# First layer's modulation tiles on VectorE and ScalarE, and branch D attention as three products of split operands

## What is computed

```
def modulate(h, shift, scale):
    return h * (1 + scale) + shift
...
        s = jnp.einsum('bhgqd,bhkd->bhgqk', qi, k).astype(jnp.float32) * scale
        p = jax.nn.softmax(s, axis=-1).astype(v.dtype)
        return jnp.einsum('bhgqk,bhkd->bhgqd', p, v)
...
    y = dense_block_attention(q, jnp.concatenate([kc, k], axis=2), jnp.concatenate([vc, v], axis=2), scale)
...
    for l in range(DEPTH):
        mod = jnp.split((sc @ ada_w[l] + ada_b[l])[:, None, :], 6, axis=-1)
        mod_c = jnp.split(scc @ ada_w[l] + ada_b[l], 6, axis=-1)
        h = modulate(rmsnorm(x, norm1_w[l]), mod[0], mod[1])
...
        x = x + mod[2] * gated_merge([ya, yb, yg, yd], p[4], w_branch[l], w_o[l])
        x = x + mod[5] * sqrelu_mlp(modulate(rmsnorm(x, norm2_w[l]), mod[3], mod[4]), mlp_w1[l], mlp_w2[l])
```

## Time and profile before

| | us |
|---|---|
| median of three runs | 2999.7 |
| their range | 2998.19 to 2999.82 |
| the profiled execution | 3000.03 |
| its span, first to last instruction | 2998.2 |

### The profile page before, as it was taken

How to read it: one execution, slowest core, us unless ns; L and a number is a source line. 1 busy time by engine, 2 the same in 40 slices (tenths; PEclk the granted TensorE clock), 3 DMA queues, 4 the chain that set the end, 5 groups by cost and what they waited for, 6 DMA issues and landing times. The chain is left out here.

```text
span 2998.2 us, 38375 instructions
## 1 busy us (share of the span) xinstructions
PE 2828.2 (94%) x15368; PEld 2308.8 (77%) x15368; DVE 1502.5 (50%) x2348; ACT 1233.9 (41%) x2155; POOL 165.9 (6%) x188
## 2 busy tenths in 40 slices
PE   6999999999999999999999999999998899999998
PEld 4887786778778778888888878777566676788887
DVE  4258753446553445664344443873446544554444
ACT  4434434434553443544233344443445544442222
POOL 0022210000000000000000000230000000000000
PEclk8999999999999999999999999999999999999999
DMA  5122231032222223243333232224031130423332
GB/s 207 57 101 96 92 138 54 22 105 76 75 84 78 67 95 120 92 141 113 112 112 112 78 107 71 84 85 138 11 96 50 43 102 22 151 85 98 93 97 91
DMA packets 84817, 273.59 MB, mean 91 GB/s; under 512 B 9520, under 2 KB 9776, under 8 KB 83888
## 3 DMA queue, kind: packets, MB, share of 16 engines
q1 hardware_dynamic: 74896, 229.84, 23.6%
q0 software_dynamic: 9760, 41.50, 4.3%
HBM read 245.07 MB, written 26.22 MB: 90 GB/s over the span
## 5 line engine op out<-in xcount | busy, mean ns | idle before, releaser
L717 PE MATMUL slot<-Hh,wh 128*128 128x512 f32 (+1 forms) x2384 | 869.9, 366 | 30.6 <-DVE wl L1849 9.2
L717 PE MATMUL slot<-Hh,wl 128*128 128x512 f32 (+1 forms) x2384 | 836.1, 352 | 0.0
L717 PE MATMUL slot<-Hl,wh 128*128 128x512 f32 (+1 forms) x2384 | 835.5, 351 | 0.0
L717 PEld LDWEIGHTS slot<-Hh,wh 128*128 128x128 f32 x2384 | 452.7, 190 | 99.0 <-issue 25.8
L1849 DVE TENSOR_TENSOR wl<-raw,wh 128x1024 fp32r<-128x1024 f32 (+1 forms) x332 | 379.6, 1144 | 289.2 <-ACT wh L1328 286.5
L1328 ACT ACTIVATE wh<-raw 128x1024 fp32r<-128x1024 f32 (+1 forms) x332 | 323.2, 974 | 435.8 <-PE slot L717 356.5
L717 PEld LDWEIGHTS slot<-Hh,wl 128*128 128x128 f32 x2384 | 452.0, 190 | 61.5
L717 PEld LDWEIGHTS slot<-Hl,wh 128*128 128x128 f32 x2384 | 453.2, 190 | 58.6 <-issue 6.0
L717 PE MATMUL slot<-Uh,wh 128*128 128x512 f32 (+1 forms) x776 | 273.9, 353 | 0.0
L717 PE MATMUL slot<-Ul,wh 128*128 128x512 f32 (+1 forms) x776 | 273.4, 352 | 0.0
L717 PE MATMUL slot<-Uh,wl 128*128 128x512 f32 (+1 forms) x776 | 273.0, 352 | 0.0
(11 more groups left out here) (258 smaller groups left out, 3847.1 us busy)
## 6 DMA issues: line engine op xcount, KB each, us to landing
raw<-w_dram SPq DMA_DIRECT2D x204, 512.0 KB, 3.5
raw<-w_gate_dram SPq DMA_DIRECT2D x64, 512.0 KB, 3.6
ada_g_raw<-ada_dram POOLq DMA_DIRECT2D x48, 512.0 KB, 3.8
ada_g_raw<-ada_dram SPq DMA_DIRECT2D x32, 512.0 KB, 3.8
raw<-w_merge_dram SPq DMA_DIRECT2D x64, 256.0 KB, 2.8
g_kept<-logits_out SPq DMA_DIRECT2D x32, 384.0 KB, 2.3
SS<-g_kept SPq DMA_DIRECT2D x32, 384.0 KB, 3.6
ada_first<-ada_dram SPq DMA_DIRECT2D x8, 1024.0 KB, 17.8
```

The costliest lines, as they stand in the source:

```text
L717: return pe.matmul(dst, lhsT, rhs, start=start, stop=stop)
```

## The change

First, `modulation_in`, `later_ada_out` and `last_column` go. Layer 0's 32 later tiles are made as layer 1's are: a product on DVE (`first_layer_product`, 128x2048) and two sums on ACT (`first_layer_sum`). They stand at the jobs of `ADA_JOBS`: ten of the C projection, the eight of the D projection, seven out-projection jobs and the first group's steps 2 to 8. The product is the first thing in DVE's `begin_job`, ahead of `low`; the sums stand behind `high` in ACT's. The condition's rows (`cs_rows`) are brought by POOL three times. Layer 1's 16 tiles of the first group move to its steps 8 to 15: one at step 8, three at step 12, two at the others.

Second, branch D's attention products are made from split operands. ACT makes high parts of each q, k and v, DVE low parts (`split_into_high`, `low_of_d`, `v_low`), and each plain product becomes three fp32r ones. Of each unit of turned probabilities ACT's copy is the high part and a new DVE subtraction, which reads the PSUM bank, the low one (`PT_LOW`, 72 units in both layers: 64 of 384 columns, 8 of 256). It stands at the head of DVE's iteration, and it, not the copy, frees the bank.

```
-        ada_prod = [at(f"ada_prod{k}", [2, D_MODEL], f32, (R_S + 7) * ROW + k * 2 * D_MODEL * 4) for k in range(2)]
+        ada_prod = [at(f"ada_prod{k}", [2, D_MODEL], f32, (R_S + 4) * ROW + (k + 1) * 2 * D_MODEL * 4) for k in range(2)]
...
-        PT["D"] = PT["B"]
+        PT["D"] = at("PT_D", [NB, SEQ], f32r, (R_S + 7) * ROW)
+        PT_LOW = [at(f"PT_low{k}", [NB // 2, SEQ], f32r, first * ROW) for k, first in enumerate((R_S, R_X + 6))]
+        KD_HIGH, KD_LOW = rows("KD_high", R_X + 2, D_KV, f32r), rows("KD_low", R_X + 4, D_KV, f32r)
+        VD_HIGH = rows("VD_high", R_X, D_KV, f32r)
+        VD_LOW = [rows(f"VD_low{k}", row, 1, f32r)[:, 0, :] for k, row in enumerate((R_S + 11, R_S + 2))]
...
-        ADA_STEPS = {"first": [x for x in range(2, 2 * KT) for _ in range(2 if x in (9, 12) else 1)],
+        FIRST_D = sum(N_PROJ[b] + LATER_GATES[0][b] + KT for b in BRANCHES[:-1])
+        ADA_JOBS = list(range(2, 10)) + [11, 12] + list(range(FIRST_D, FIRST_D + KT)) + list(range(FIRST_FF - KT, FIRST_FF - 1))
+        ADA_JOBS += list(range(FIRST_FF + 2, FIRST_FF + KT + 1))
+        assert len(ADA_JOBS) == N_GATE
+
+        ADA_STEPS = {"first": [x for x in range(KT, 2 * KT) for _ in range({KT: 1, 12: 3}.get(x, 2))],
...
                 tile(src, raw, raw_full, jobs % 2, size)
+                if jobs - 1 in ADA_JOBS:
+                    ada_tile(ADA_JOBS.index(jobs - 1))
...
+            def ada_tile(t):
+
+                sp.wait_ge(ada_read.sem, ADA_FIRST + max(t - 1, 0))
+                sp.dma_start(ada_g_raw[t % 2][:, :, :], w_ada[ADA_FIRST + t]).then_inc(ada_g_full[t % 2].sem, 16)
...
-                        if j > 0:
-                            ada_tile(layer, len(gate_jobs) - 2)
...
-                        if x == 0:
-                            ada_tile(layer, len(gate_jobs) - 1)
...
+            def condition_rows():
+
+                rows_in = cs_kept.rearrange("s p k -> s (p k)").unsqueeze(0).to_broadcast([P, 2, D_MODEL])
+                pool.dma_start(cs_rows[:, :, :], rows_in).then_inc(cs_back.sem, 16)
...
+                if layer == 0:
+                    pool.wait_ge(cs_packed.sem, w.next(cs_packed))
+                    for side in range(2):
+                        pool.dma_start(cs_kept[side], cs[:, side * KT:(side + 1) * KT]).then_inc(cs_saved.sem, 16)
+                    pool.wait_ge(cs_saved.sem, w.next(cs_saved, 2))
+                    pool.wait_ge(mod_done.sem, w.next(mod_done, FIRST_PIECES))
+                    condition_rows()
...
+                        if layer == 0 and after == BRANCHES[-1]:
+                            condition_rows()
...
-                            pool.dma_start(cs_rows[:, :, :], rows_in).then_inc(cs_back.sem, 16)
+                            condition_rows()
...
-            def modulation_in(dst, full, tile):
-
-                pe.wait_ge(full.sem, w.next(full))
-                for k in range(KT):
-                    strip = slice(32 * (k % 4), 32 * (k % 4 + 1))
-                    last = mm(dst[strip, :], cs_wide[:, k, :], tile[:, k, :], start=k < 4, stop=k >= 4)
-                last.then_inc(ada_read.sem, 1)
...
-                    if part == 1:
-                        modulation_in(later_ada, ada_g_full[g % 2], ada_g_raw[g % 2])
-                        if g > 0:
-                            mm(later_cols, mod_g_t[(g - 1) % 2][:, :], sel)
...
-                        transposes(beside, slot[beside], VT[branch][j % 2], NB, copied).then_inc(tr_done.sem, 1)
+                        transposes(beside, slot[beside], VT[branch][j % 2], NB, v_low if branch == "D" else copied).then_inc(tr_done.sem, 1)
...
+                            if branch == "D" and tile["first"] and len(tile["keys"]) == NB and h % (D_HEADS // D_KV) == 0:
+                                pe.wait_ge(d_low.sem, w.next(d_low, 1 if h else D_SPLITS - 1))
...
-                                    last = mm(out_s[:, lo:hi], QY[:, h, qs_], KD[:, h // (D_HEADS // D_KV), lo:hi])
+                                    kv = h // (D_HEADS // D_KV)
+                                    mm(out_s[:, lo:hi], Yh[:, h, qs_], KD_HIGH[:, kv, lo:hi], start=True, stop=False)
+                                    mm(out_s[:, lo:hi], Yl[:, h, qs_], KD_HIGH[:, kv, lo:hi], start=False, stop=False)
+                                    last = mm(out_s[:, lo:hi], Yh[:, h, qs_], KD_LOW[:, kv, lo:hi], start=False, stop=True)
...
-                        pe.wait_ge(pt_ready.sem, w.next(pt_ready, values_in))
+                        pe.wait_ge(turned.sem, w.next(turned, values_in))
+                        if branch == "D" and i - LAG - 1 == LB - 1:
+                            pe.wait_ge(v_low.sem, w.next(v_low, D_KV))
...
-                                last = mm(values_at[:, 0:tile["width"]], V[:, tile["h"] // 2, m * P:(m + 1) * P], pt, **flags)
+                                kv, block = tile["h"] // (D_HEADS // D_KV), slice(m * P, (m + 1) * P)
+                                dst, low = values_at[:, 0:tile["width"]], PT_LOW[x // 3][:, x % 3, 0:tile["width"]]
+                                mm(dst, VD_HIGH[:, kv, block], pt, start=x == 0, stop=False)
+                                mm(dst, VD_LOW[kv][:, block], pt, start=False, stop=False)
+                                last = mm(dst, VD_HIGH[:, kv, block], low, start=False, stop=flags["stop"])
...
-                            pe.wait_ge(*slots.next(("unit", units % 2), pt_ready))
+                            pe.wait_ge(*slots.next(("unit", units % 2), turned))
...
-                if layer == 0 and branch == BRANCHES[-1]:
-                    last_column()
...
+                first_layer_sum(layer, n)
...
-                    if layer == 0:
-                        later_ada_out(later)
...
+                    if branch == "D":
+                        dst = Yh[:, j, 0:nq] if kind == "q" else KD_HIGH[:, j, :]
+                        act.activation(dst, src[:, 0:nq] if kind == "q" else src, ACT.Copy).then_inc(d_high.sem, 1)
+                        return
...
+                        split_before = branch == "B" and n > 0 or branch == "D" and n > 2
+                        p = begin_job(between=(lambda: split_into_high(*plan[n - (3 if branch == "D" else 1)])) if split_before else None)
...
+                        if branch == "D":
+                            act.activation(VD_HIGH[:, j, :], slot[beside][:, 0:T], ACT.Copy).then_inc(v_high.sem, 1)
...
+                    split_into_high(*plan[D_SPLITS - 1])
...
+            def first_layer_sum(layer, n):
+
+                if layer or n not in ADA_JOBS:
+                    return
+                t = ADA_JOBS.index(n)
+                act.wait_ge(ada_read.sem, w.next(ada_read, 1 + (0 if t else ADA_FIRST)))
+                for side in range(2):
+                    row = ada_prod[t % 2][:, side, :]
+                    ins = act.activation(row, row, ACT.Copy, accum_out=mod[:, ADA_FIRST + t, side:side + 1])
+                ins.then_inc(ada_summed.sem, 1)
+
...
+                        if first:
+                            first_layer_sum(layer, n + x)
...
+                first_layer_product(layer, n)
                 if n > min(layer, 1):
...
+                        if branch == "D" and n > 2:
+                            between = lambda: low_of_d(nq, *plan[n - 3])
...
+                    if branch == "D" and n > 0 and plan[n - 1][0] == "v":
+                        j = plan[n - 1][1]
+                        dve.wait_ge(v_high.sem, w.next(v_high))
+                        dve.tensor_tensor(VD_LOW[j], slot[1 + 2 * ((n - 1) % 2)][:, 0:T], VD_HIGH[:, j, :].bitcast(f32),
+                                          ALU.subtract).then_inc(v_low.sem, 1)
+                if branch == "D":
+                    low_of_d(nq, *plan[D_SPLITS - 1])
+
+            def low_of_d(nq, kind, j):
+
+                dve.wait_ge(d_high.sem, w.next(d_high))
+                if kind == "q":
+                    ins = dve.tensor_tensor(Yl[:, j, 0:nq], QY[:, j, 0:nq], Yh[:, j, 0:nq].bitcast(f32), ALU.subtract)
+                else:
+                    ins = dve.tensor_tensor(KD_LOW[:, j, :], KD[:, j, :], KD_HIGH[:, j, :].bitcast(f32), ALU.subtract)
+                ins.then_inc(d_low.sem, 1)
...
+                    if branch == "D" and LAG < i <= len(tiles) + LAG:
+                        tile = tiles[i - LAG - 1]
+                        for lo, hi in key_units(tile):
+                            span = slice(tile["col"], tile["col"] + P)
+                            dve.wait_ge(pt_high.sem, w.next(pt_high))
+                            dve.tensor_tensor(PT_LOW[lo // 3][:, 0:hi - lo, span],
+                                              unit_bank(units)[:, 0:(hi - lo) * P].rearrange("p (b s) -> p b s", s=P),
+                                              PT["D"][:, lo:hi, span].bitcast(f32), ALU.subtract).then_inc(pt_low.sem, 1)
+                            units += 1
                     for j, part in over:
...
```

(20 more changed lines are left out.)

113 lines of the change are left out of this document (40 added, 73 removed).

## The result

The change made the kernel slower by 0.33%, where the prediction had 2992.4 us and a range up to 3004.

The account below looks back on a forecast made before the run. The prediction took PE, busy for 94% of the span, as the bound. C -7.8, A -2.3, B -5.5, last column -0.2, D +1.6 and +2.5, feed-forward +4.4 gave -7.3, so 2992.4 us, range 2977 to 3004.

Parts of the forecast that it names:

- The sum by its own terms: All predicted changes of the whole kernel's time added up: -7.3 us.
- 9 of 17 gates paying: Branch C: modulation off PE saves time only in gates not followed by a PE wait; C -7.8 us in all.
- my 2.3 and 5.5: Modulation taken off PE saves 2.3 us in branch A and 5.5 us in branch B.
- The ring: Branch D attention: ACT's exponential and copies, DVE's subtractions and row maximum form a loop of 3.56 us a tile.
- the later start: Branch D: first scores come later through added products, sums and splits, +4.1 us in layer 0, +1.1 in layer 1.
- my +2.5: Branch D attention of layer 1, later start included: +2.5 us.
- +1.4: Layer 0 from D to out-projection: +1.6 us for D, -0.2 for the last column.
- +4.4: First feed-forward group: steps fall behind through the moved products, +4.4 us, bounds 1 and 8.
- The slower one: Rival in D attention: each subtraction costs the ring more, at 0.80 us D gives +23.1, time 3011 us; chance 0.10.
- The third: Rival: half of the modulation's gain of 15.6 us is off the path, time 3000.2 us; chance 0.20.

Follow-up runs that it names:

- modulation alone: The kernel before with only the first part of the change, modulation tiles on DVE and ACT, branch D attention as before: 2996.42 us, ratio 0.9986.
- Filling C's waits: Useless PE products ahead of branch C's waits in layer 0, added to the changed kernel (3001.55 us, 1.0009) and to the modulation alone (2986.39 us, 0.9956).
- the kernel with less PE work in C: The kernel before with most of PE's modulation products in branch C of layer 0 left out, DVE and ACT unchanged: 2997.11 us, ratio 0.9986.
- The split alone: The kernel before with only the second part of the change, branch D attention from split operands, modulation as before: 3010.90 us, ratio 1.0053.

## Why the prediction was wrong

**The step that failed** is the first: "a microsecond off PE's program is a microsecond off the time, wherever PE does not then wait for something else". It goes with a second sentence: "Before such a wait a shorter PE only waits longer." I counted a wait that grows as worth nothing, neither gain nor loss, and so put the clock at nothing. Here it was a loss: behind the longer waits PE ran on at 0.5. The sum by its own terms (-7.3) was near what the trace shows without the clock (-11.9); the clock added 20 in the profiles, and 19 over the runs by the estimate above.

**C.** 9 of 17 gates paying gave -7.8; the mixer's work and waits together are -6.7 in the kernel after and -7.0 with the modulation alone. That was right within 1 or 2 us. The wait that I read as 2.09 us grew to 3.12 at each of three heads. Filling C's waits gave 7 and 9 us, so what followed from their growth cost about that much; the falls of the clock behind them are what the filling took away.

**A and B.** Work fell by 3.4 and 7.4, a little more than my 2.3 and 5.5, and B kept it. In A the two waits of 2.04 and 2.31 us were there before, ended by nothing that the profile names ("issue"). Rows of the kernel before and of the kernel after, then the stretch from the first of them, in the same order:

```profile
517.45 1.10 PE L717 MATMUL slot<-XS,QY 128*128 128x512 f32 x2 [2.04 <-issue]
...
521.99 0.47 PE L717 MATMUL slot<-Hh,wh 128*128 128x512 f32 x1 [2.31 <-issue]
```
```profile
517.32 1.10 PE L730 MATMUL slot<-XS,QY 128*128 128x512 f32 x2 [2.04 <-issue]
...
522.62 0.76 PE L730 MATMUL slot<-Hh,wh 128*128 128x512 f32 x1 [2.31 <-issue]
```
```profile
517.40:522.00 4.60, 2.24 (x9) 1.48 (x9) 2.32 (x3) 0.99 (x2) 0.00 (x0) 1.00 0.24 57
```
```profile
517.30:522.00 4.70, 2.99 (x8) 1.92 (x8) 2.29 (x3) 0.47 (x1) 0.00 (x0) 0.64 0.22 56
```

The same two waits, the clock at 1.00 in one execution and 0.64 in the other. The two programs differ between the waits, but the kernel with less PE work in C has the A of the kernel before, and in its profile the clock was at 0.5 from 1.3 us behind the first of the same two waits to 3 us behind the second. So a given wait brings a fall sometimes, and part of A's +5.6 is chance: in the profiles of this case with the modulation off PE, A has from 1.6 to 7.1 us of clock. It goes with this that runs of one kernel spread over 10 us and more, the slower ones mostly with the lower clock (modulation alone: 2987.26 at 0.989, 2998.89 at 0.984).

**D attention.** The ring was priced right. The subtraction took 552 ns for 384 columns where I had put 0.55, and 424 for 256:

```profile
L2324 DVE TENSOR_TENSOR PT_low<-slot,PT_D 128x384 fp32r<-128x384 f32 x64 | 32.7, 552 | 24.8 <-ACT PT_D L1686 24.5
L2324 DVE TENSOR_TENSOR PT_low<-slot,PT_D 128x256 fp32r<-128x256 f32 x8 | 3.4, 424 | 16.3 <-ACT PT_D L1686 16.2
```

The 525 ns that I worked out from the Trainium skill's page VectorE: DVE Perf Modes, section on the TRN2 errata, is 5% too low here; the measurement decides. From one exponential to the next the ring is 3.52 us (3.56 predicted), and 5.21 where a gate ends, with high and low of the next tile in it:

```profile
2497.95 0.91 ACT L1701 ACTIVATE SS<-slot,negmax 128x768 f32<-128x768 f32 x1 [1.76 <-DVE negmax L2341]
...
2501.47 0.91 ACT L1701 ACTIVATE SS<-slot,negmax 128x768 f32<-128x768 f32 x1 [1.27 <-DVE negmax L2341]
...
2506.68 0.90 ACT L1701 ACTIVATE SS<-slot,negmax 128x768 f32<-128x768 f32 x1 [2.52 <-DVE negmax L2341]
```

The first two value products of layer 1 stay 18.1 us apart (18.3 before) though PE's work between them shrank, as said. In layer 1 work and waits give +2.4 with the later start, against my +2.5. What was missing is clock, +6.8, behind waits such as these, the second at the end of a gate:

```profile
2484.42 0.56 PE L730 MATMUL slot<-KD_high,Yh 128*128 128x512 f32 x1 [2.55 <-DVE VD_low L2107]
```
```profile
2505.28 0.45 PE L1221 MATMUL slot<-ident,SS 128*128 128x128 f32 x1 [2.54 <-DVE PT_low L2324]
```
```profile
2505.20:2508.60 3.40, 3.32 (x11) 2.97 (x12) 2.62 (x7) 1.75 (x4) 0.00 (x0) 0.51 0.31 77
```

Before, the first scores of layer 1 waited 1.10 us, and no stretch of that layer's D attention was below 1.0. How much of +9.1 they are differs between executions. The split alone runs the same program in this layer: its profile has the same waits of 2.55 and 2.55 us, each followed by a fall, then none where the kernel after has two more, and D attention at +5.2 (waits +9.1, clock +3.4). So up to half of the clock's +6.8 is this execution's. In the eight profiles without the value product's split this layer's D attention has 0 to 1.7 us of clock, in the six that have it whole and its start not filled, 3.4 to 13.2. No experiment took the clock away while leaving the waits.

In layer 0 work and waits are -0.5 against +1.4, clock +5.2. The later start was priced right: PE's wait ahead of the last transposes grew from 0.9 to 4.1 us (I had 3.0 more), that ahead of the first scores from 1.1 to 2.5 (1.1 more).

```profile
992.34 0.41 PE L933 MATMUL slot<-ident,XS 128*128 128x128 f32 x2 [4.08 <-DVE SS L2043]
```

**The first feed-forward group** had +4.4 and got +5.1, in part by luck: waits are +3.2, and the clock, which I had not counted, is +1.7. PE stood once for 3.17 us, behind the step with three products, and not by 0.5 to 1 us a step as I had said. The third product waited 2.19 us for its tile to be brought, where I had put 0.5 for its buffer and its tile:

```profile
1323.81 2.29 DVE L2383 TENSOR_TENSOR ada_prod<-cs_rows,ada_g_raw 128x2048 f32<-128x2048 f32 x1 [2.19 <-DMA ada_g_raw<-ada_dram]
```
```profile
1330.59 0.51 PE L730 MATMUL slot<-Uh,wh 128*128 128x512 f32 x1 [3.17 <-DVE wl L1853]
```

**The rivals.** The slower one had the wrong mechanism (a dearer subtraction). The third had its sign, a stretch of C as long as before (-0.1), but not for its reasons: about as many gates paid as were counted, and the clock took what they gave. The chance of 0.12 for slower was too low because all of my cases were counted at one clock. The Trainium skill's page TensorE: Matmul & The Clock Gate, section on HAM oscillation, describes a kernel in which PE waits for the next slice of an operand to be brought, and each of these waits sends it back to its lower clock. I had not weighed it. Read that way, the longer waits of C and D would have been a price, and the trace agrees with it in kind; it shows also that waits of 2 us do so in one execution and not in another, while those of 3.12 us did each time.

## What to carry to other kernels

When you take work off the busiest engine, look at what it waits for next. If that wait was already long, the removed work was covering it, and the wait grows by all of it. On PE a grown wait isn't free: read the granted clock behind it before and after, and where the next engine can't be made faster, a few useless products ahead of the wait can be worth more than the work that was removed. A new subtraction that frees a bank is both in the ring and the release of another engine's next step, so it can't be moved by looking at the ring alone.

## What was not expected of the hardware

- Two waits of 2.04 and 2.31 us, the same in both kernels, were followed by a granted clock of 1.00 in one execution and 0.64 over the stretch in another.
- At one place (the end of C's first head) the clock held behind waits of 0.43, 1.78, 2.09 and 2.57 us, fell behind one of 2.07 in another kernel's profile, and fell with each of seven of 3.12 us.
- Over 80 runs of one kernel, time follows the lost clock: 0.72 us more for each us lost, correlation 0.92.
- 15 us of 3009 hung on 0.26 us in each of 64 subtractions (0.552 against 0.290) and half of that in 8 more.
